# First norm summed by token thirds and spread by TensorE, bias line in four column groups of 256

## What is computed

```
def rmsnorm(x, g):
    xf = xf * lax.rsqrt(jnp.mean(xf * xf, axis=-1, keepdims=True) + EPS)
    return (xf * g.astype(jnp.float32)).astype(x.dtype)
...
def rglru_mixer(x, h0, conv_buf, positions, w_in, conv_w, conv_b, w_a, b_a, w_x, b_x, lam, w_out):
    u = x @ w_in
    gate_branch, rec = u[..., :D_RNN], u[..., D_RNN:]
    x_full = jnp.concatenate([conv_buf.astype(rec.dtype), rec], axis=1)
    xc = causal_dwconv(x_full, conv_w, conv_b)
    r = jax.nn.sigmoid(block_diag(xc, w_a, b_a).astype(jnp.float32))
    i = jax.nn.sigmoid(block_diag(xc, w_x, b_x).astype(jnp.float32))
...
        bias = jnp.transpose(jnp.take(rel_bias, rel_bucket(rel), axis=0), (2, 0, 1))
        s = jnp.where((rel >= 0)[None, None, None], s + bias[None, :, None], NEG_INF)
```

## Time and profile before

| | |
|---|---|
| time of the kernel before, median of 3 runs | 2472.62 us (2472.5 to 2473.6) |
| time of the profiled execution | 2473.61 us |
| its span | 2471.4 us |
| TensorE (PE) busy | 2446.7 us, 99% of the span |
| VectorE (DVE) busy | 1864.0 us, 75% |
| ScalarE (ACT) busy | 1074.5 us, 43% |
| GpSimd (POOL) busy | 288.5 us, 12% |
| granted TensorE clock, mean | 0.998 of full speed |

### The profile page before, as it was taken

The page is one execution under the profiler, slowest core; times in us unless marked ns, Lnnn a source line. Parts: engine busy times, 40 slices in busy tenths (PEclk is TensorE's granted clock), DMA queues, the critical chain, the costliest instruction groups (busy, mean ns, idle before and its releaser), DMA issues.

```text
span 2471.4 us, 45466 instructions
## 1 busy us (share of the span) xinstructions
PE 2446.7 (99%) x18016; PEld 2390.3 (97%) x18016; DVE 1864.0 (75%) x2914; ACT 1074.5 (43%) x2034; POOL 288.5 (12%) x171
## 2 busy tenths in 40 slices
PE   8999999999999999999999999999999999999998
PEld 7999999999999999998999999899999999999998
DVE  8877498777778777886655555648877777778788
ACT  5765164333333333434444444625433333333333
POOL 2001300000000000043333333021000000000001
PEclk9999999999999999999999999999999999999999
DMA  4111414555555555434233332422355555555542
GB/s 148 50 45 58 134 53 154 182 187 184 190 185 192 192 188 188 149 140 132 89 97 100 99 98 97 152 62 75 136 187 184 192 192 189 192 184 172 189 157 105
DMA packets 151169, 352.08 MB, mean 142 GB/s; under 512 B 17285, under 2 KB 55685, under 8 KB 150702
## 3 DMA queue, kind: packets, MB, share of 16 engines
q1 hardware_dynamic: 145006, 326.88, 39.4%
q10 hardware_dynamic: 5952, 22.30, 2.4%
HBM read 236.76 MB, written 117.07 MB: 143 GB/s over the span
## 4 chain that ended last, share of the span: by engine, by line
PE 93%; DVE 4%; issue 1%; ACT 1%; DMA 0%; SPq 0%; DVEq 0%; ACTq 0%
PE psum L1458 20%; PE psum L1331 12%; PE psum L1335 12%; PE psum L1333 12%; PE psum L1185 11%; PE psum L1520 4%; PE psum L1524 3%; PE psum L1522 3%; PE psum L1166 3%; PE psum L1554 2%; PE psum L1578 2%; PE psum L1755 2%; PE psum L1566 1%; DVE line L2505 1%; PE psum L1319 1%
## 5 line engine op out<-in xcount | busy, mean ns | idle before, releaser
L1331 PE MATMUL psum<-xn_hi,w_hi 128*128 128x264 f32 x1472 | 417.9, 284 | 0.0
L1333 PE MATMUL psum<-xn_hi,w_lo 128*128 128x264 f32 x1472 | 417.8, 284 | 0.0
L1335 PE MATMUL psum<-xn_lo,w_hi 128*128 128x264 f32 x1472 | 417.2, 283 | 0.0
L1458 PE MATMUL psum<-h_hi,w_lo 128*128 128x352 f32 x1032 | 333.2, 323 | 0.0
L1458 PE MATMUL psum<-h_hi,w_hi 128*128 128x352 f32 x1032 | 332.1, 322 | 0.2 <-DVE x L2866 0.2
L1458 PE MATMUL psum<-h_lo,w_hi 128*128 128x352 f32 x1032 | 332.2, 322 | 0.0
L1331 PE MATMUL psum<-s_hi,w_hi 128*128 128x264 f32 x1104 | 314.5, 285 | 0.4 <-DVE w_lo L767 0.4
L1335 PE MATMUL psum<-s_lo,w_hi 128*128 128x264 f32 x1104 | 314.6, 285 | 0.0
L1333 PE MATMUL psum<-s_hi,w_lo 128*128 128x264 f32 x1104 | 313.1, 284 | 0.0
L1335 PEld LDWEIGHTS psum<-xn_lo,w_hi 128*128 128x128 f32 x1472 | 277.0, 188 | 0.0
L1331 PEld LDWEIGHTS psum<-xn_hi,w_hi 128*128 128x128 f32 x1472 | 276.6, 188 | 0.3
(11 more groups left out here) (395 smaller groups left out, 5990.6 us busy)
## 6 DMA issues: line engine op xcount, KB each, us to landing
scratch_x<-x SPq DMA_DIRECT2D x168, 528.0 KB, 5.1
x<-scratch_x SPq DMA_DIRECT2D x168, 528.0 KB, 4.6
w_raw<-in_w SPq DMA_DIRECT2D x192, 256.0 KB, 4.9
w_raw<-in_w SPq DMA_DIRECT2D x56, 512.0 KB, 3.7
w_raw_third<-in_w SPq DMA_DIRECT2D x96, 256.0 KB, 4.6
k_pages<-in_cache_k SPq DMA_DIRECT2D x128, 64.0 KB, 2.0
v_pages<-in_cache_v SPq DMA_DIRECT2D x128, 64.0 KB, 2.1
scratch_line<-scratch_row ACTq DMA_DIRECT2D x1, 4608.0 KB, 21.3
```

What stands on the lines that cost most here:

```text
L1331: pe.matmul(out, op_hi(op)[:, k, :], hi[k][:, cols], start=start and k == 0, stop=False, skip_group_check=True)
L1333: pe.matmul(out, op_lo(op)[:, k, :], hi[k][:, cols], start=False, stop=False, skip_group_check=True)
L1335: last = pe.matmul(out, op_hi(op)[:, k, :], lo[k][:, cols], start=False, stop=True, skip_group_check=True)
L1458: last = pe.matmul(PS[:, z + c, 0:CH], w[:, k, :], r[:, c * CH:(c + 1) * CH], start=first, stop=end)
```

## The change

`norm_sum(0)` is replaced by two functions on PE. `first_sums` sums each third of 352 tokens into one group of 32 PSUM partitions of bank 6. ACT's `root(0)` then works on 96 partitions by 352 columns, into the tile `roots_in_sum_line` (SROOT), and DVE's `first_inverse` takes the reciprocal there. `first_spread`, put ahead of the last eighth of unit 1, spreads the thirds with five matmuls into banks 6, 7 and 2. ACT copies the first 704 columns from there into `inverse_rms`, DVE the other 352 (`first_copies`). `bias_line` now writes four groups of 256 columns into four groups of 8 PSUM partitions of bank 6, once those copies are made. ACT copies that as 104 partitions by 256 columns, and writes it to HBM with four DMAs and a fifth for the 128 constant columns behind it, in place of one DMA.

```diff
-            def norm_sum(r):
-                z, y, lo = 6, 2, CH
-                pe.wait_ge(sum_done, (KT - 1) * (r + 1))
-                pe.matmul(PS[:, z, :], ONES[:, :], Z[2][:, 0:512], start=True, stop=True)
-                pe.matmul(PS[:, z + 1, :], ONES[:, :], Z[2][:, 512:SEQ], start=True, stop=True)
-                pe.matmul(PS[:, y, lo:lo + TS], ONES[:, :], Z[2][:, SEQ:T], start=True, stop=True
-                          ).then_inc(sum_mm, 1)
+            def first_sums():
+                pe.wait_ge(sum_done, KT - 1)
+                for c in range(NCH):
+                    last = pe.matmul(PS[32 * c:32 * (c + 1), 6, 0:CH], ONES[:, 0:32],
+                                     Z[2][:, c * CH:(c + 1) * CH], start=True, stop=True)
+                last.then_inc(sum_mm, 1)
+
+            def first_spread():
+                pe.wait_ge(pick_set, 1 + QUARTERS)
+                pe.wait_ge(root_done, 2)
+                wait_read(pe, acc_rec(0))
+                for i, (c, out, lo, n) in enumerate(first_pieces()):
+                    if i == 2:
+                        pe.wait_ge(line_mm, 2)
+                    rows = slice(32 * c, 32 * (c + 1))
+                    last = pe.matmul(out, PICK[rows, :], SROOT[rows, lo:lo + n], start=True, stop=True)
+                    if i < 2:
+                        last.then_inc(line_mm, 1)
+                last.then_inc(line_mm, 1)
...
             def bias_line():
-                pe.wait_ge(root_done, 2)
+                pe.wait_ge(line_read, 2)
...
-                for c in range(2):
-                    last = pe.matmul(PS[0:NH, 6 + c, :], TAB[:, :], HOT[:, c * 512:(c + 1) * 512],
+                for j in range(QUARTERS):
+                    last = pe.matmul(PS[32 * j:32 * j + NH, 6, 0:QT], TAB[:, :], HOT[:, j * QT:(j + 1) * QT],
                                      start=True, stop=True)
...
             first(0, range(4, KT))
-            norm_sum(0)
-            first(1, range(4, KT))
+            first_sums()
+            first(1, range(4, KT - 1))
+            first_spread()
+            first(1, (KT - 1,))
             bias_line()
...
             def root(r):
-                z, y, lo = 6, 2, CH
                 act.wait_ge(sum_mm, r + 1)
-                act.activation(RINV[:, 0:SEQ].rearrange("p (b t) -> p b t", b=2), PS[:, z:z + 2, :],
-                               ACT.Sqrt, bias=EPSC[:, :], scale=1.0 / D).then_inc(root_done, 1)
-                act.activation(RINV[:, SEQ:T], PS[:, y, lo:lo + TS], ACT.Sqrt, bias=EPSC[:, :],
-                               scale=1.0 / D).then_inc(root_done, 1)
+                act.activation(SROOT[0:32 * NCH, :], PS[0:32 * NCH, 4 if r else 6, 0:CH], ACT.Sqrt,
+                               bias=EPSC[0:32 * NCH, :], scale=1.0 / D).then_inc(root_done, 2 if r else 1)
...
-                act.wait_ge(line_mm, 1)
-                act.activation(BLN[:, 0:SEQ].rearrange("h (c n) -> h c n", c=2), PS[0:NH, 6:8, :],
-                               ACT.Copy, scale=-1.0).then_inc(line_read, 1)
-                act.wait_ge(line_read, 1)
+                rows = 32 * (QUARTERS - 1) + NH
+                act.wait_ge(line_mm, 4)
+                act.activation(BLN[0:rows, :], PS[0:rows, 6, 0:QT], ACT.Copy, scale=-1.0).then_inc(line_read, 1)
+                act.wait_ge(line_read, 3)
                 act.wait_ge(dve_const, 3)
-                act.dma_start(S["row"], BLN[:, :]).then_inc(row_out, 16)
+                for j in range(QUARTERS):
+                    act.dma_start(S["row"][:, j * QT:(j + 1) * QT], BLN[32 * j:32 * j + NH, :]).then_inc(row_out, 16)
+                act.dma_start(S["row"][:, SEQ:LINE], BLT[:, :]).then_inc(row_out, 16)
...
             root(0)
             raw(0)
+            act.wait_ge(line_mm, 3)
+            act.activation(RINV[:, 0:2 * CH].rearrange("p (b t) -> p b t", b=2), PS[:, 6:8, 0:CH], ACT.Copy
+                           ).then_inc(line_read, 1)
             raw(1)
...
-            def inverse(r):
-                dve.wait_ge(root_done, 2 * r + 2)
-                step(dve.reciprocal(RINV[:, :], RINV[:, :]))
+            def first_inverse():
+                dve.wait_ge(root_done, 1)
+                dve.reciprocal(SROOT[0:32 * NCH, :], SROOT[0:32 * NCH, :]).then_inc(root_done, 1)
+
+            def first_copies():
+                b = SEQ - 2 * CH >> 1
+                dve.wait_ge(line_mm, 3)
+                dve.wait_ge(line_read, 1)
+                dve.tensor_copy(RINV[:, 2 * CH:SEQ].rearrange("p (b t) -> p b t", b=2), PS[:, 6:8, CH:CH + b])
+                dve.tensor_copy(RINV[:, SEQ:T], PS[:, 2, CH:CH + TS]).then_inc(line_read, 1)
+                dve.wait_ge(line_read, 2)
...
+            first_inverse()
             dve.wait_ge(act_const, 1)
...
-            inverse(0)
+            first_copies()
```

More of the change, by code:

```diff
@@ L1817, in root @@
             def root(r):
-                if r:
-                    act.wait_ge(sum_mm, r + 1)
-                    act.activation(SROOT[0:32 * NCH, :], PS[0:32 * NCH, 4, 0:CH], ACT.Sqrt,
-                                   bias=EPSC[0:32 * NCH, :], scale=1.0 / D).then_inc(root_done, 2)
-                    return
-                z, y, lo = 6, 2, CH
                 act.wait_ge(sum_mm, r + 1)
-                act.activation(RINV[:, 0:SEQ].rearrange("p (b t) -> p b t", b=2), PS[:, z:z + 2, :],
-                               ACT.Sqrt, bias=EPSC[:, :], scale=1.0 / D).then_inc(root_done, 1)
-                act.activation(RINV[:, SEQ:T], PS[:, y, lo:lo + TS], ACT.Sqrt, bias=EPSC[:, :],
-                               scale=1.0 / D).then_inc(root_done, 1)
+                act.activation(SROOT[0:32 * NCH, :], PS[0:32 * NCH, 4 if r else 6, 0:CH], ACT.Sqrt,
+                               bias=EPSC[0:32 * NCH, :], scale=1.0 / D).then_inc(root_done, 2 if r else 1)
             def norm_after_units(l, r, a0, gain, released):
```

15 lines of the change are left out of this document (10 added, 5 removed).

## The result

The changed kernel took 2476.03 us (median of 22 runs, 2473.81 to 2478.63), the kernel before 2473.22 us in the same comparison (22 runs, 2471.94 to 2474.21): a ratio of 1.0013, 95% interval 1.0007 to 1.0018. That is 2.8 us more, slower by less than 0.2%, and just outside the range forecast. The profiled execution took 2477.77 us.

A forecast was written before the change was run, and what follows sets the result against it. TensorE, busy 2446.7 of 2471.4 us, was taken as the bound. PE would be ready at 49.5 us but `xc_lo` only at 51.1, so `diag(0)` starts 0.9 us later: 2473.5 us from a median of 2472.62, range 2471.6 to 2475.9 us.

The forecast's parts named there:

- the place where three engines meet: PE's hole of 0.39 us at 49.90 us before `diag(0)`; PE, ACT and DVE start anew from 50.29 us.
- the sums: First norm on PE: three column groups take 0.73 us instead of 1.96 us, a gain of 1.23 us.
- the spread: New PE work ahead of the last nine matmuls of unit 1: 2.0 us with its small gaps.
- the reciprocal that POOL doesn't hold up: DVE's first reciprocal starts at once despite POOL's weight split, takes 2.35 us; rival that POOL holds it up: chance 0.06.
- ACT's five issues decide: Five DMA issues ahead of ACT's tap put it at 43.1 us instead of 42.17: +0.9 us at `diag(0)`.
- the clock falls: Rival: PE's hole growing to 1.6 us brings half speed behind it; +3.1 us, 2475.7 us; chance 0.13.
- The step of an issue: ACT's time from one DMA issue to the next before the tap: 0.5 us, bounds 0.36 and 0.67 us.
- So the 4.5 us that the reciprocal gives back go into waiting for ACT: Before the convolution: unit 0 is scaled by 38.5 or 41 us, before ACT comes to its tap.
- The DVE side no longer decides: Before the convolution: `inverse_rms` is ready at 37.1 us instead of 40.08, so DVE doesn't set the tap's start.
- the gain comes through: Rival: issues don't hold ACT, PE alone decides, `diag(0)` at 49.5 to 50.0 us; -0.3 to -0.8 us; chance 0.17.
- Everything behind it moves as a block: All work after `diag(0)` shifts by the same 0.9 us as `diag(0)` itself, up to the kernel's end.
- after it PE leads and its waits are a tenth or two each: Behind the meeting at 50.29 us, the change's effect on the end is its shift there, to a few tenths.

The follow-up runs named there:

- run 1: Changed kernel with the five DMA issues of the bias rows moved behind the first convolution tap: 2475.65 us against 2473.11 (ratio 1.0012).
- run 8: Kernel before with the bias line's row DMA in seven pieces instead of one, ahead of the first tap: 2474.18 us (1.0005).
- run 4: Changed kernel with one more wait on GpSimd, so that VectorE goes first at 227 us: 2474.94 us (1.0009).
- run 5: Changed kernel with two more waits on GpSimd, so that VectorE goes first at 212 and 227 us: 2474.86 us against 2472.86 (1.0008).
- run 16: Changed kernel with VectorE forced first at 212 and 227 us and 24 fulfilled waits on SyncE: 2474.90 us (1.0009).
- run 15: Changed kernel with 24 fulfilled waits on SyncE ahead of the reads of `xn_lo` near 1557 us: 2475.77 us (1.0011).
- run 9: Kernel before with two waits on GpSimd that put VectorE first at 212 and 227 us: 2473.51 us against 2473.32 (1.0002).
- Run 13: Changed kernel with a GpSimd wait that puts VectorE first at 212 us only, 227 us left free: 2476.15 us against 2473.07 (1.0011).
- run 2: Norm part of the change alone, bias line with its copy and DMA as in the kernel before: 2474.79 us (1.0009).
- run 7: Kernel before with two waits on VectorE, so that GpSimd goes first at 212 and 227 us: 2474.87 us (1.0009).
- Run 18: Kernel before with 26 more fulfilled waits on TensorE ahead of `diag(0)`: 2473.80 us against 2473.10 (1.0003).
- run 17: Changed kernel with DMA issues behind the tap, VectorE forced first at 212 and 227 us, 24 waits on SyncE: 2474.41 us against 2472.96 (1.0005).
- run 3: Bias part of the change alone (four column groups, five DMAs), norm as in the kernel before: 2474.87 us (1.0008).
- run 14: Kernel before with a VectorE wait that puts GpSimd first at 212 us only, 227 us left free: 2473.73 us (1.0002).

## Why the prediction missed

**Right.** The bound, the place where three engines meet, the sums, the spread and the reciprocal that POOL doesn't hold up; that ACT's five issues decide, shown by runs 1 and 8, though by 0.7 us only; the hole of 1.64 us and a meeting point 0.84 us later. The rival "the clock falls" was wrong in its place: the hole stands in a row of the chain, and the granted clock stayed at 1.00 behind it.

**Mis-sized, without effect.** The step of an issue is 0.39 us, not 0.5; a gap of 0.54 us before DVE's convolution, 0.11 us in before, made up for it. Its cause was not tried.

**Wrong, and hidden by the issues.** "So the 4.5 us that the reciprocal gives back go into waiting for ACT": DVE waited 1.01 us ahead of its convolution. "The DVE side no longer decides" held by 0.46 us only. Its `softplus_tmp` row took 4.12 us instead of 1.36, next to POOL's split, and with the gap of 0.35 us that followed it in run 1 it would have set the convolution at 43.8 us by itself, an estimate from these rows. Run 1 shows the same: with the issues out of the way `diag(0)` starts at 50.44 us. The rival "the gain comes through" has 49.5 to 50.0 us for that case, which left this row out too.

**The step that failed**, and made the time miss, is "Everything behind it moves as a block", with its ground, "after it PE leads and its waits are a tenth or two each". It took PE's waits for the whole of what the engines do to each other, and left out that DVE and POOL, released together, hold each other up in an order that can turn. What the runs showed in its place:
- The first stage gives 0.8 to 1.1 us (three profiles of after against the first of before; run 8, +1.07 us in the mean span).
- The order at 212 and 227 us gives 1.4 to 2.0 us: +2.0 us where it is forced upon before, together with the waits that force it. Put back in after (runs 4, 5 and 16, mean span 2472.7 us, against 2473.6 of after and run 15) it gives 0.9 us, and 0.5 us more if the waits' own cost by run 9 is taken off. The clock behind it is within this. Run 13 isn't in that mean: DVE was first twice in its profile too, and its mean span is only 0.4 us below after's. With 11 runs each and spans that scatter by about 1 us, this size is known to some half a microsecond, not better.
- The late read and the stretch at 1.2 GHz near 1573 us give between nothing (run 2) and 3 us (run 13) in single profiles. The stretch alone, without a late read, gave 0.7 to 0.8 us (runs 1, 7, 15). Over all runs, what is left of the mean span of after (2473.8 against 2471.0 us) when the first two are taken off is -0.3 to +0.6 us, so its average share is not settled. That the fetch beside SP's third issue is what delays it is argued from twenty profiles, not shown by an edit that takes it away.
- At the kernel's end all kernels run at 1.2 GHz. In before's first profile that begins at 2463.2 us, in after's at 2470.9 us. The shift was +4.9 us up to there and +4.2 at PE's last matmul, so this gave 0.7 us back.
- Outside the span, time less span was, in the means of the kernels, 1.8 to 2.1 us in those without the norm part and 2.1 to 2.5 us with it (mean 1.95 and 2.3): some 0.35 us that no row shows. Run 18, which is before with waits on PE, had 2.3 us too. Open.

**The chances.** The forecast of no change within 0.2% held, since 2.8 us is 0.11%. That is no merit of the mechanism, which accounts for about a third of the loss. The range failed: its upper end, 2475.9 us, took in the meeting point and one fall of the clock, but nothing for an order that turns later. The forecast stood on the median of three runs, 2472.62 us; the 22 runs of the comparison gave 2473.22 us, and that 0.6 us alone is more than the 0.13 us by which the range was missed. The range failed by little, and the step failed by 2 us.

No kernel of this study beat before. The best version with all of the change, run 17, came to 2474.41 us against 2472.96, and its interval, 0.9996 to 1.0014, includes no change.

## What to carry to other kernels

Where two engines can hold each other up and are released by one event, a shift is not the end of a forecast: look in the trace for pairs whose starts lie within some tens of nanoseconds, price the other order (here 1.4 to 2 us), and add it to the range, or fix the order with a wait if the good one is known. DMA issues stand in an engine's own queue: five of them ahead of a tap took 0.37 to 0.39 us each. Before you credit an engine with the time that a shorter instruction frees, look at what else it does in that time: here small DVE steps, moved next to a GpSimd split, took 4.12 us instead of 1.36, and came within 0.5 us of deciding. And judge a change of a tenth of a per cent by several profiles of both kernels: three profiles of one program had spans from 2473.8 to 2475.8 us.

## What the runs showed of the hardware that was not expected

- POOL and DVE were released together at 212 us. Where DVE's start was recorded 13 or 14 ns behind POOL's (four profiles), POOL was held up; where it was 19 to 25 ns behind (eight profiles), DVE was.
- A DVE step of 8 elements per partition (`softplus_tmp`), 0.17 us long otherwise, took 2.34 us beside a GpSimd tensor by tensor operation of 2.38 us.
- The same waits of PE (0.45, 0.62, 0.82, 0.69 and 1.05 us, between 1563 and 1573 us) were followed by a stretch at 1.2 GHz in some kernels' profiles and not in others: in run 1 from 1571.9 us for 3.4 us, in run 7 from 1573.8 us, in run 2 none.
- A hole of 1.64 us behind a long busy stretch left the granted clock at 1.00, a wait of 1.9 us with a few matmuls before and after was followed by 3.4 us at 1.2 GHz in three profiles, all of after. Waits of 1.9 us at the same place in runs 3, 14 and 15, and one of 2.1 us in run 7, were not.
- The third issue of a DMA on SP near 1557 us came 0.35 to 0.9 us late in the twelve profiles in which a fetch of instructions on another queue ran beside it, and in none of the eight without.
